# The first output projection's units become steps of the mixers' weave, by quarters of their input

## The reference, cut to what matters

```python
z = rmsnorm(h, norm_mix_g[l]) @ w_in[l]                      # 256 x 3840
a_q, a_f, a_i, a_g, b_q, b_k, b_v, c_in = jnp.split(z, splits, axis=-1)
o_a = hgrn2_mix(a_q, a_f, a_i, a_g, lbs[l], hgrn_gnorm_g[l])  # 512 columns
o_b = dilated_window_mix(b_q, b_k, b_v)                       # 256 columns
o_c, v_first = rwkv7_mix(c_in, ...)                           # 256 columns
h = h + jnp.concatenate([o_a, o_b, o_c], axis=-1) @ w_out[l]  # 1024 x 1024
h = h + conv_glu_ffn(rmsnorm(h, norm_ffn_g[l]), ...)          # the next stage
```

## Time and profile before

| | us |
|---|---|
| median of 3 runs | 1687.3 |
| lowest and highest run | 1680.6, 1694.55 |
| the profiled execution's own time | 1693.7 |
| its span in the trace | 1691.9 |
| of it: mixers' weave, first dense product to last matmul | 18.5 to 264.9 |
| from there to the first matmul of w_out | 264.9 to 276.87 |
| products of w_out | 276.87 to 299.15 |

### The profile page before, as it was taken

How to read it: one execution, slowest core, us unless ns; L and a number is a source line. 1 busy time by engine, 2 the same in 40 slices (tenths; PEclk the granted TensorE clock), 3 DMA queues, 4 the chain that set the end, 5 groups by cost and what they waited for, 6 DMA issues and landing times.

```text
span 1691.9 us, 31871 instructions
## 1 busy us (share of the span) xinstructions
PE 1610.2 (95%) x10694; PEld 1465.3 (87%) x10694; DVE 1191.8 (70%) x2272; ACT 866.0 (51%) x1594; POOL 334.5 (20%) x248
## 2 busy tenths in 40 slices
PE   7899998999998988999999899999999999999997
PEld 7789977999887887888999899997888899999996
DVE  3777665788755567645469758878999767676776
ACT  4655434665556633555554555554444544545454
POOL 2334220011100332032028655540000000000000
PEclk9899999999999989999999999999999999999999
DMA  7433244455663620053546554446777665656564
GB/s 255 124 88 112 86 127 137 145 186 164 195 195 117 233 75 1 9 187 117 162 142 207 174 153 142 144 139 215 243 240 241 204 188 185 189 186 186 186 186 149
DMA packets 88137, 271.36 MB, mean 160 GB/s; under 512 B 9856, under 2 KB 26624, under 8 KB 87680
## 3 DMA queue, kind: packets, MB, share of 16 engines
q1 hardware_dynamic: 65088, 237.01, 45.4%
q10 hardware_dynamic: 22976, 33.36, 6.2%
HBM read 258.80 MB, written 11.53 MB: 160 GB/s over the span
## 4 chain that ended last, share of the span: by engine, by line
PE 79%; DVE 11%; ACT 5%; issue 3%; DMA 1%; POOL 1%; ACTq 1%; DVEq 0%; SPq 0%; POOLq 0%
PE ps_chunk L481 42%; PE ps_misc L481 20%; PE ps_misc L290 8%; PE ps_chunk L290 4%; PE ps_misc L2302 3%; DVE w_lo L423 1%; ACT w_hi L416 1%; DVE ffn_arena L1438 1%; PE ps_misc L696 1%; DVE mixers_arena L2107 1%; DVE mixers_arena L2108 1%; DVE mixers_arena L2104 1%; POOL w_lo L423 1%; DMA raw<-in_stream 1%; DVE mixers_arena L2103 1%
## 5 line engine op out<-in xcount | busy, mean ns | idle before, releaser
L416 ACT ACTIVATE w_hi<-raw 128x512 fp32r<-128x512 f32 (+1 forms) x900 | 548.5, 626 | 501.6 <-PE ps_chunk L481 299.1
L423 DVE TENSOR_TENSOR w_lo<-raw,w_hi 128x512 fp32r<-128x512 f32 x682 | 496.2, 744 | 275.6 <-ACT w_hi L416 265.9
L481 PE MATMUL ps_chunk<-x_hi,w_hi 128*128 128x256 f32 x1856 | 543.6, 293 | 22.8 <-POOL w_lo L423 10.2
L481 PE MATMUL ps_chunk<-x_hi,w_lo 128*128 128x256 f32 x1856 | 529.5, 285 | 0.0
L481 PE MATMUL ps_chunk<-x_lo,w_hi 128*128 128x256 f32 x1856 | 529.2, 285 | 0.0
L423 POOL TENSOR_TENSOR w_lo<-raw,w_hi 128x512 fp32r<-128x512 f32 (+2 forms) x218 | 284.1, 1318 | 554.8 <-ACT w_hi L416 480.2
L481 PEld LDWEIGHTS ps_chunk<-x_hi,w_hi 128*128 128x128 f32 x1856 | 359.8, 194 | 35.1 <-POOL w_lo L423 16.0
L481 PEld LDWEIGHTS ps_chunk<-x_hi,w_lo 128*128 128x128 f32 x1856 | 360.3, 194 | 2.9 <-issue 0.2
L481 PEld LDWEIGHTS ps_chunk<-x_lo,w_hi 128*128 128x128 f32 x1856 | 359.6, 194 | 0.0
L481 PE MATMUL ps_misc<-w_hi,hid_hi 128*128 128x512 f32 x520 | 205.1, 394 | 5.9 <-DVE w_lo L423 5.9
L481 PE MATMUL ps_misc<-w_hi,hid_lo 128*128 128x512 f32 x520 | 204.3, 393 | 0.0
(11 more groups left out here) (344 smaller groups left out, 1767.8 us busy)
## 6 DMA issues: line engine op xcount, KB each, us to landing
raw<-in_stream SPq DMA_DIRECT2D x452, 512.0 KB, 3.6
early_rows<-row ACTq DMA_DIRECT2D x64, 128.0 KB, 2.5
row<-early_rows ACTq DMA_DIRECT2D x64, 128.0 KB, 3.9
memory_kv<-mixers_arena ACTq DMA_DIRECT2D x4, 512.0 KB, 3.7
mixers_arena<-in_cmp_w ACTq DMA_DIRECT2D x1, 2048.0 KB, 7.6
mixers_arena<-memory_kv ACTq DMA_DIRECT2D x4, 512.0 KB, 6.1
mixers_arena<-in_consts ACTq DMA_DIRECT2D x1, 1665.0 KB, 10.5
row<-in_rows ACTq DMA_DIRECT2D x3, 512.0 KB, 7.3
```

Source lines behind the costliest of these rows:

```text
L416: e.activation(w_hi[q % 2][:, s], raw[q][:, s], ACT.Copy).then_inc(made, 1)
L423: e.tensor_tensor(w_lo[q % 2][:, s], raw[q][:, s], w_hi[q % 2][:, s].bitcast(F32), ALU.subtract).then_inc(made, 1)
L481: last = e.matmul(o, stationary[a], moving[b], start=start and i == 0, stop=stop and i == 2, skip_group_check=True)
```

## The change

- The weave's strand `dense_chunks` goes on after mem_v with `woven_projection("w_out", LAST_QUARTER_LAST, ...)`: the eight units of w_out are steps of the weave, in the order (0,0) (0,1) (1,0) (1,1) (0,2) (1,2) (0,3) (1,3). The stream's units are laid out in the same order.
- The strand of `hgrn` and `windows` loads x again after `windows` and then turns (transposes) columns 0 to 511 and 512 to 767 of `mixed` into x, for each half of the tokens, once mem_v's last chunk is out of PSUM. The strand of `rwkv` does so with columns 768 to 1023 when it has ended. A product of chunk 12 waits for its quarter of x.
- `woven_projection` takes the order of units as an argument; the sum for the left half of the columns (`first_half`) is issued after unit (0,3), that is behind the seventh of eight units. It was behind the sixth of eight in `BY_HALVES`.
- The fence, the 14 matmuls before the transposes, `feature_major` and `add_projection("w_out")` go. All lanes still wait for each other's last counted instruction after the weave.
- `MIXERS_ORDER` is a new string of 425 letters: 242 d, 86 r, 86 h, 11 m.
- Unit 0 of ffn_up is still split ahead; unit 1 is now split by the loop of `ffn`.

The core of the diff:

```diff
-MIXERS_ORDER = ("dmdddddddddddddddddddddddddddddddddddddmrrddrddddrrrdmmrdddddrddrddddddddrddddrdddhhdrhdddrdhrhrdddd"
...
+MIXERS_ORDER = ("ddddddmdddddddddddddddddddddddddmddddddrrdddrddddrddddrdddrdddddrddrdddmrddddhhhdddrdddhdhddhdrddhdh"
...
+LAST_QUARTER_LAST = ((0, 0), (0, 1), (1, 0), (1, 1), (0, 2), (1, 2), (0, 3), (1, 3))
-        split_up_to, dense_end, dense_number = [0], [UNITS * STREAM["w_out"][0] + 1], {}
+        split_up_to, dense_end, dense_number = [0], [UNITS * STREAM["ffn_up"][0] + 1], {}
-        def woven_projection(name, x_parts, *needs):
+        def woven_projection(name, order, x_parts, needs):
             first, _ = STREAM[name]
+            end_0 = order.index((0, UNITS - 1)) + 1
...
-                e.wait_ge(s_use, first * UNITS + 6)
+                e.wait_ge(s_use, first * UNITS + end_0)
...
-            for i, (chunk, q) in enumerate(BY_HALVES):
+            for i, (chunk, q) in enumerate(order):
                 u, n = first * UNITS + i, first + chunk
                 woven_split(u)
                 for part in range(2):
                     for some in range(2):
                         if chunk == 0:
                             yield
-                            while (q // 2, some) not in x_parts:
+                            while (q, some) not in x_parts:
                                 yield "early"
-                            pe.wait(*x_parts[q // 2, some])
+                            pe.wait(*x_parts[q, some])
+                        if q == 0 and part == 0 and some == 0:
+                            pe.wait(*banks.free[n % 2 * 2], *banks.free[n % 2 * 2 + 1])
                         woven_products(u, n, q, part, some, True, ps_chunk[n % 2], ((s_ev, n - 1),) * 2, lambda k: ())
                         if (part, some) == (0, 0):
                             woven_split(u + 1)
-                        if i == 6 and (part, some) == (0, 1):
+                        if i == end_0 and (part, some) == (0, 1):
                             dve.wait(*needs)
                             dve.quiet(first_half)
...
+        def part_of_x(src, first_q, count, t, x_parts):
...
+            made_x = turn([src[:, t, k * P:(k + 1) * P] for k in range(2 * count)], [dve.now()], evac)
+            for q in range(first_q, first_q + count):
+                x_parts[q, t] = made_x
...
+            yield from woven_projection("w_out", LAST_QUARTER_LAST, x_parts, x_again)
...
         def hgrn_and_windows():
             yield from hgrn()
             yield from windows()
+            x_again.append(load("x_again", h[:, :, :], x.rearrange("(t p) n -> p t n", p=P), pe.now(), dve.now(), act.now()))
+            yield
+            yield from evacuated(mem_multiplied, act, dve)
+            for t in range(TT):
+                part_of_x(mixed, 0, 2, t, x_parts)
+                yield
+            for t in range(TT):
+                part_of_x(mixed[:, :, 512:768], 2, 1, t, x_parts)
+                yield
+
+        def rwkv_to_x():
+            yield from rwkv()
+            yield
+            yield from evacuated(mem_multiplied, act, dve)
+            for t in range(TT):
+                part_of_x(mixed[:, :, 768:1024], 3, 1, t, x_parts)
+                yield
...
-        act.wait((s_kv[0], 32), (s_kv[1], 32))
+        ends = [lane.now() for lane in work] + [(s_kv[0], 32), (s_kv[1], 32)]
+        for lane in work:
+            lane.wait(*ends)
         dve.wait((s_lo1, dense_end[0]))
-        fence()
-        x_again = load("x_again", h[:, :, :], x.rearrange("(t p) n -> p t n", p=P))
...
-        keep_warm(14)
-        t = feature_major(mixed, plain, [dve.now()])
-        dve.wait(x_again)
-        added = add_projection("w_out", t)
+        added = added_by["w_out"]
```

More of the change, by code:

```diff
@@ L848, in woven_projection @@
                             woven_split(u + 1)
-                        if i == 6 and (part, some) == (0, 1):
+                        if i == end_0 and (part, some) == (0, 1):
                             dve.wait(*needs)
                             dve.quiet(first_half)
-                        if i == 6 and (part, some) == (1, 1):
+                        if i == end_0 and (part, some) == (1, 1):
                             act.quiet(first_squares)
@@ L859, in build @@
         added_by = {}
-        def half_of_x(src, half, t):
+        def part_of_x(src, first_q, count, t, x_parts):
             def evac(ps, done):
-                hi, lo = (a[:, 4 * half:4 * half + 4, t * P:(t + 1) * P] for a in (x_hi, x_lo))
+                hi, lo = (a[:, 2 * first_q:2 * (first_q + count), t * P:(t + 1) * P] for a in (x_hi, x_lo))
                 ps = ps.rearrange("p (k n) -> p k n", n=P)
@@ L867, in evac @@
                 return (dve.do(lambda e: e.tensor_tensor(lo, ps, hi.bitcast(F32), ALU.subtract), a, own=False),)
-            return turn([src[:, t, k * P:(k + 1) * P] for k in range(4)], [dve.now()], evac)
+            made_x = turn([src[:, t, k * P:(k + 1) * P] for k in range(2 * count)], [dve.now()], evac)
+            for q in range(first_q, first_q + count):
+                x_parts[q, t] = made_x
         def normed_x(gain, added, *bias_made, warm=12):
@@ L1378, in dense_chunks @@
                               (s_ev, n + 1))
+            yield from woven_projection("w_out", LAST_QUARTER_LAST, x_parts, x_again)
+        x_parts, x_again = {}, []
+        mem_multiplied = STREAM["w_out"][0]
         def hgrn_and_windows():
@@ L1382, in hgrn_and_windows @@
             yield from windows()
-        weave(MIXERS_ORDER, dense=(0, 2, dense_chunks()), rwkv=(4, 4, rwkv()), hgrn=(2, 2, hgrn_and_windows()),
+            x_again.append(load("x_again", h[:, :, :], x.rearrange("(t p) n -> p t n", p=P), pe.now(), dve.now(), act.now()))
[14 more added lines that the diff above has]
+                yield
+        weave(MIXERS_ORDER, dense=(0, 2, dense_chunks()), rwkv=(4, 4, rwkv_to_x()), hgrn=(2, 2, hgrn_and_windows()),
               memory=(0, 2, memory_tokens()))
-        act.wait((s_kv[0], 32), (s_kv[1], 32))
+        ends = [lane.now() for lane in work] + [(s_kv[0], 32), (s_kv[1], 32)]
+        for lane in work:
+            lane.wait(*ends)
         dve.wait((s_lo1, dense_end[0]))
-        fence()
-        x_again = load("x_again", h[:, :, :], x.rearrange("(t p) n -> p t n", p=P))
         plain = lambda k: c("one")
         sp_out = [0]
-        keep_warm(14)
-        t = feature_major(mixed, plain, [dve.now()])
-        dve.wait(x_again)
-        added = add_projection("w_out", t)
+        added = added_by["w_out"]
         def ffn(added):
@@ L1650, in dense_chunks @@
                                  func=lambda n: ACT.Sigmoid if n == first + 4 else ACT.Copy)
-                yield from woven_projection("w_out_2", x_parts, *normed_ends)
+                yield from woven_projection("w_out_2", BY_HALVES, x_parts, normed_ends)
             def begin():
@@ L1774, in layer_norm @@
                 made_x = into_x(SF, 0, plain, [act.now()])
-                for t in range(TT):
-                    x_parts[0, t] = made_x
+                for part in ((0, 0), (0, 1), (1, 0), (1, 1)):
+                    x_parts[part] = made_x
                 yield
@@ L2021, in dense_chunks @@
                 yield from dense(q_first, 2, False, lambda n: four(QM)(n - q_first), by_k=t, pairs=2)
[L2022 removed]
+                yield from woven_projection("mem_o", BY_HALVES, x_parts, ())
             def two_heads(pair, t):
@@ L2554, in token_units, with in_order @@
     return full.reshape(UNITS, 2, P, n, CW).transpose(3, 0, 2, 1, 4).reshape(-1, P, UNIT)
-def by_halves(units):
-    return units[[UNITS * chunk + q for chunk, q in BY_HALVES]]
+def in_order(units, order):
+    return units[[UNITS * chunk + q for chunk, q in order]]
 def lay_out(a):
@@ L2569, in lay_out @@
     parts["w_in token"] = token_units(np.concatenate([ai, ag, bv], 1))
-    parts["w_out"] = token_units(a["w_out"][0])
+    parts["w_out"] = in_order(token_units(a["w_out"][0]), LAST_QUARTER_LAST)
     up = a["ffn_up"][0].reshape(D, 2, NF // 2, 2 * P).transpose(0, 2, 1, 3).reshape(D, 2 * D_FF)
@@ L2578, in lay_out @@
         [token_units(w[:, lo:lo + CW]) for lo in (3 * CW, 4 * CW, 2 * CW)])
-    parts["w_out_2"] = by_halves(token_units(a["w_out_2"][0]))
+    parts["w_out_2"] = in_order(token_units(a["w_out_2"][0]), BY_HALVES)
     for n, units in (("q", feature_units), ("k", feature_units), ("v", token_units), ("o", token_units)):
         parts["mem_" + n] = units(a["w_mem_%s_2" % n][0])
-    parts["mem_o"] = by_halves(parts["mem_o"])
+    parts["mem_o"] = in_order(parts["mem_o"], BY_HALVES)
     parts["peer_q"] = feature_units(a["peer_w_q_2"][0])
```

12 lines of the change are left out of this document (6 added, 6 removed).

## The result

The changed kernel takes 1696.93 us (median of 20 runs, 1689.43 to 1702.77) against 1685.41 for the kernel before in the same rounds (20 runs): a ratio of 1.0062, 95% interval 1.0046 to 1.0078, or 10.5 us slower (7.8 to 13.1). The forecast was no change, -2.1 us. So the sign was another, and 1696.93 lies just above 1696, the slowest case of the prediction.

The account below looks back on a forecast made before the run. PE, busy 95% of the span, was taken as the bound; -10.1 + 2.6 + 2.2 + 3.2 = -2.1 us gave 1685.2 us against the 1687.3 median, forecast as no change (0.85 within 1%), cases reaching from 1671 to 1696.

Parts of the forecast that it names:

- The barrier, -10.1: Between weave and w_out: 11.97 us without products go, 1.91 us of transposes come back inside the weave; -10.1 us.
- Half clock, put at nothing outside the barrier: After hgrn's start: half clock taken as before, 3.1 us, 0 to 3.1 more or less possible.
- hgrn's start: Before hgrn's first level: PE stands 7.2 us against 5.5 of old holes, +1.7, with a split wait +1.9.
- The new order's holes, +3.2: Rest of the weave under the new string: hgrn's start +1.9 and hgrn's levels +1.3; later parts counted as nothing.
- 12 steps in place of 8: Behind rwkv's reciprocal: 12 dense steps where 8 stood, four being 2.8 us, so the 2.59 us hole closes by itself.
- The joints, +2.2: Two places inside the weave where w_out's x is made ready, (a) 1.2 and (b) 1.0: +2.2 us.
- (a): Joint where mem_v's last sums leave PSUM before x is overwritten and chunk 12 begins: 1.2 us uncovered (0.3 to 2).
- (b): Joint where x's last quarter needs rwkv's end: need 9.5 to 12 us, cover 10.7, taken at 1.0 (0 to 1.5).
- Contention at (b): DVE and POOL locking each other out at rwkv's end; by the skill's rule 1 us more, weighed but not counted.
- The tail, +2.6: Behind w_out: second sum 1.3 us later, less 0.4 for splits, plus 1.7 waiting for ffn's unit 1; 1 to 4.
- hgrn starves PE: Rival, first to fifth hgrn level: holes and half clock +8.7, in all +4.7 us, 1692; chance 0.25.
- The signs named beforehand: Trace signs: products end near 294.5, L831 1.3 us later, ffn wait 1.7, hgrn's hole 3 or more, with prior wait 7.

Follow-up runs that it names:

- e6: Changed kernel with 18 identity matmuls ahead of the eight matmuls of hgrn's first level; 1.0035 of the kernel before.
- e5: Changed kernel with 18 in place of 12 identity matmuls ahead of ffn's scaling; 1.0059 of the kernel before.
- e12: Kernel before with 12 identity matmuls in its hole at 55 and 10 in that at 73; 1.0000 of the kernel before.
- e15: e10 with identity matmuls in the holes at 55 and 73, and six more ahead of the transposes of rwkv's result; 0.9981 of the kernel before.
- e1: Changed kernel with the old order string's first 214 letters, then the new string's steps not yet done; 1.0030 of the kernel before.
- e2: Kernel before, barrier included, with the new string's first 206 letters, then the old string's remaining steps; 1.0049 of the kernel before.
- e4: Changed kernel with the left half's sum issued ahead of ffn unit 0's split and unit 1 split in the weave; 1.0017 of the kernel before.
- e9: Changed kernel with the edits of e4 and e6 together; 1.0002 of the kernel before.
- e3: Changed kernel with the whole old order string and the new steps behind it; 1.0055 of the kernel before.
- e10: Changed kernel with the edit of e4 and the old first letters of e1; 0.9995 of the kernel before.
- e8: Changed kernel with hgrn's exponential, logarithm, sigmoid and silu before its first level replaced by absolute values; 1.0035 of the kernel before.
- e14: Changed kernel run and profiled once more, unchanged; 1.0069 of the kernel before.
- e7: Changed kernel with six dense steps moved from late in the string to just ahead of hgrn's first level; 1.0158 of the kernel before.

## Why the prediction was wrong

By idle time, half clock and work, the forecast up to the last product was +1.3, -2.9 and -3.1 (the barrier's 4.1 idle, 2.9 half clock and 5.0 work less the transposes, then 5.4 of new holes), and the runs show +3.4, +2.5 and -2.7. In the tail it was +2.6 in all and the runs show +3.0 idle and +3.4 half clock. Of the 11.7 us by which the first tap was missed, 8.8 are half clock by the profiles' rows. Timed runs confirm that share only in part: with half clock taken away by identity matmuls alone e6 gained 4.6 us, and e5, e12 and e15 nothing that shows. That the early letters and the tail make up the loss is shown by timed runs (e1, e2, e4, e9).

- **The barrier, -10.1: gone, but not kept.** e1, e3 and e10 have the old early order without the barrier, and are 0.2 to 1.0 us ahead of before at the last product where -10.1 + 2.2 would be 7.9. Holes at the joints (3.01 and 2.16 in e3) and, in e1 and e10, at 163 to 171 fill the idle again, and half clock comes elsewhere where the barrier had 2.8 us of it. Only the identity matmuls, 2.7 us of work, are saved for good. I counted the barrier's half clock as saved.
- **Half clock, put at nothing outside the barrier: the step that failed.** The sum books the barrier's 2.9 us of half clock as saved, says of hgrn's start "The half clock after it I take as before", and has no such term for any other new hole or for the tail: -2.9 in all. Measured are +2.5 up to the last product and +3.4 in the tail. At hgrn's start "as before" came true: 2.7 at 81 to 92, where the two profiles of before have 3.1 and 3.4 between 71 and 92. But the spell at 54 costs 1.3 more than before, now that 1.27 us of idle follow the 3.17, and the one at 102, behind a hole that the sum hasn't, 1.7. The two at 225 and 290 cost 5.1, about what the late spells of before cost with the barrier's (4.6 and 6.1): there nothing was saved. The tail's 3.4 stand behind its two waits, and e4, which shortens them, has none.
- **The new order's holes, +3.2: the mechanism right, the size short by 2 us.** hgrn's start was foreseen at 7.2 and measured at 2.30 + 4.74 = 7.04, with ACT and DVE as the cause (e8). That a hole closes by "12 steps in place of 8" was wrong in kind: the 2.30 us behind rwkv's reciprocal stayed, since the DVE half of a unit waits for it, in every order run here (2.59 in the old, 2.30 in the new). The levels cost less than thought (0.4 at one, against 1.4 before), but 1.27 at 55.4, 1.69 at 101.6 and 2.37 at 164.8 were not in the sum. "The rows show no idle of note there and I count nothing" failed: rows of the old order can't show the holes of the new. And the prediction's list of the largest holes leaves out the largest, at 55, by PE's timeline of before:

```profile
55.22 3.79 PE L290 MATMUL ps_misc<-mixers_arena 64*128 64x256 f32 x12 [3.17 <-ACT mixers_arena L1112]
```

- **The joints, +2.2: the sum right, the shares not.** The first, (a), cost 0.21 where I had 1.2; the second, (b), 1.59 + 0.16 = 1.75 where I had 1.0, at most 1.5.
- **Contention at (b): it came.** On DVE, between the end of rwkv's matmuls and the transposes, two operations take 1.67 us where their like take 0.69, each while POOL is making a low part. First DVE's timeline, then POOL's:

```profile
283.52 1.67 DVE L1332 TENSOR_TENSOR mixers_arena<-mixers_arena,row 128x512 f32<-128x512 f32 x1
285.22 0.69 DVE L1333 TENSOR_TENSOR mixers_arena<-mixers_arena,row 128x512 f32<-128x512 f32 x1
285.94 1.67 DVE L1334 TENSOR_TENSOR mixers_arena<-mixers_arena 128x512 f32<-128x512 f32 x1
```

```profile
283.12 1.52 POOL L425 TENSOR_TENSOR w_lo<-raw,w_hi 128x512 fp32r<-128x512 f32 x1 [1.07 <-ACT w_hi L418]
285.62 1.44 POOL L425 TENSOR_TENSOR w_lo<-raw,w_hi 128x512 fp32r<-128x512 f32 x1 [0.98 <-ACT w_hi L418]
```

  One such operation stood there before, so the moved splits added one, 0.98 us. With it (b) would have been forecast at 2.0, nearer to the 1.75 than my 1.0. By the rule of the Trainium skill ("SBUF — State Buffer", who interferes with whom) that I weighed and set aside, this trace agrees. The row by which I set it aside, the low part of 0.69 us at 724.98, was no test of it: POOL's own low part ended at 725.01 (POOL's timeline of before), so the two hardly met.

```profile
723.72 1.29 POOL L423 TENSOR_TENSOR w_lo<-raw,w_hi 128x512 fp32r<-128x512 f32 x1 [1.42 <-ACT w_hi L416]
```

- **The tail, +2.6: waits right, clock missing.** The second sum's delay was foreseen at 0.9 net and is 1.1; the wait for unit 1 was foreseen at 1.7 and is 1.91 (2.04 in e14). The two pauses then brought 3.4 us of half clock in both profiles of the changed kernel and none in either of before. e4 took all of it out and gained 7.6.
- **The rival "hgrn starves PE"** (0.25) was right in kind, slower by holes and half clock, and not in place. From 60 us to hgrn's fifth level PE is idle for 9.8 us (7.2 before) and its spells cost 4.5 (3.3 before): +3.8, under its condition of 5.3 and far under its +8.7. The rest of the loss lies outside its place, at 54, 164.8 and in the tail, which it left at full clock.
- **The signs named beforehand:** hole and wait before it 7 (7.04), ffn's wait 1.7 (1.91), second sum 1.3 behind the products (302.67 against 301.39): right. Products' end at 294.5: wrong, 301.4. That should have gone with a sum of its own for the clock. Three terms are slightly off as written and move nothing: the tail's chain adds up to 4.2 and not 4.1, joint (a) leaves 2.5 - 1.5 = 1.0 and not 1.2, and hgrn's first level began 11.0 us behind chunk 3 and not 11.1.

Open: which letters open the holes at 163 to 171 wasn't tried, and where a spell without a hole before it (at 225, 200 or 250) will fall can't be told from these runs.

## What to carry to other kernels

A hole in the bounding engine has two prices, its length and the half clock behind it (here 1.7 us, or twice that, behind most of the holes listed); count the second for every hole that is new or longer, and don't book a barrier's half clock as saved. When a barrier goes, look at what it let the next stage have ready (here a split unit and a sum at once), and move that too. Before filling a hole by moving work ahead, follow the operands of that work: if they are made on the engine that causes the hole, it only grows (e7).

## What the hardware showed that I had not expected

- The granted clock can fall with no idle at all. In the changed kernel PE was busy for 4.94 of 5 us from 225 to 230 at 0.52, behind some 6 us in which small matmuls (64 by 64, then 64 by 128) alternate with dense steps; e14 has it at the same place (0.59).

```profile
225.00:230.00 5.00, 4.94 (x16) 0.52 0.36 105
```

- The same idle doesn't always cost the clock: 2.37 us at 164.8 was followed by 1.00 (the same hole in e6, 2.36 at 162.0, by a spell of 1.7), 1.69 at 101.6 by 0.66, and 1.6 ahead of ffn's scaling by full clock in three profiles and by half in four.
- ACT's tables cost their load of 1.28 us and nothing beside it (77.01 + 1.28, next function at 78.30), as in the trace of before. With the drain of 1.38 us a switch that "ScalarE: Activation LUTs" (what ACT_TABLE_LOAD costs) of the Trainium skill adds, e8 would have taken over 10 us off ACT's chain; it took off 5.2, which is the four loads and 0.1 more (75.94 to 86.56, then 75.14 to 80.55).
